# Layer 0's modulation additions redistributed over TensorE, VectorE and w_out, unused columns left unsplit, and the last head's maximum placed ahead of a split

## The reference

```
for l in range(2):
    mod = silu(c) @ w_ada[l] + b_ada[l]                 # 2048 x 6144
    shift, scale, gate = split(mod, 3)
    h = layernorm(x) * (1 + scale) + shift
    u_f, z_f, cq, ckv, k_r, z_a = split(h @ w_in[l])
    y_f = fourier_mix(u_f, w_fmix[l]) * silu(z_f)       # 8 groups of 128
    q, k, v from rmsnorm(cq) @ w_q_b[l], rmsnorm(ckv) @ w_kv_b[l], rope
    y_a = softmax(q k / sqrt(192)) v * silu(z_a)        # 8 heads
    y = concat(y_f, y_a) @ w_out[l]
    x = layernorm(alpha * x + gate * y, ln_g[l], ln_b[l])
```

## Time and profile before

| | |
|---|---|
| Median of 3 runs | 2102.82 us (2100.85 to 2103.71) |
| The profiled execution | 2105.26 us, its span 2103.5 us |
| PE busy | 96% of the span |
| DVE busy | 66% |
| ACT busy | 44% |
| DMA | 219 GB/s from and to HBM over the span |
| Layer 0, from its last Fourier groups to the turn into layer 1 | about 200 to 478 us of the span |

### The profile page before, as it was taken

The page is one execution under the profiler, slowest core; times in us unless marked ns, Lnnn a source line. Parts: engine busy times, 40 slices in busy tenths (PEclk is TensorE's granted clock), DMA queues, the critical chain, the costliest instruction groups (busy, mean ns, idle before and its releaser), DMA issues.

```text
span 2103.5 us, 36631 instructions
## 1 busy us (share of the span) xinstructions
PE 2026.9 (96%) x14264; PEld 1842.2 (88%) x14264; DVE 1378.0 (66%) x1891; ACT 934.9 (44%) x1390; POOL 29.7 (1%) x59
## 2 busy tenths in 40 slices
PE   5999999988999999899999999999999999999998
PEld 1788898768999987899999998889889889989986
DVE  5457677786788867888997555565455545545555
ACT  2344455444545644433346335454334434434443
POOL 0000000000000000000000000000000000000000
PEclk8999999999999999999999999999999999999999
DMA  9988888874577565344545555544545555555553
GB/s 366 397 332 315 311 317 312 320 260 172 199 258 256 224 219 196 122 180 168 184 168 181 201 184 194 200 159 181 200 181 184 195 195 184 180 199 182 190 189 138
DMA packets 64403, 462.40 MB, mean 220 GB/s; under 512 B 7264, under 2 KB 7808, under 8 KB 8368
## 3 DMA queue, kind: packets, MB, share of 16 engines
q1 hardware_dynamic: 57152, 410.49, 53.1%
q0 software_dynamic: 7152, 50.51, 6.5%
HBM read 458.85 MB, written 2.13 MB: 219 GB/s over the span
## 4 chain that ended last, share of the span: by engine, by line
PE 68%; DVE 7%; ACT 2%; issue 1%; DVEq 0%; ACTq 0%
PE ps L523 22%; PE ps L524 22%; PE ps L525 22%; DVE w_lo L1697 2%; DVE area L1733 1%; ACT w_hi L1149 1%; PE ps L565 1%; DVE st L1717 1%; ACT sc L1403 0%; ACT sc L1409 0%; DVE X L2174 0%; DVE grow L2271 0%; DVE csil L2118 0%; DVE area L2271 0%; ACT area L1531 0%
## 5 line engine op out<-in xcount | busy, mean ns | idle before, releaser
L1697 DVE TENSOR_TENSOR w_lo<-raw,w_hi 128x1024 fp32r<-128x1024 f32 x642 | 758.5, 1221 | 390.0 <-ACT w_hi L1149 387.0
L1149 ACT CAST w_hi<-raw 128x1024 fp32r<-128x1024 f32 (+1 forms) x642 | 640.8, 1047 | 457.3 <-PE ps L525 440.8
L523 PE MATMUL ps<-a_hi,w_lo 128*128 128x256 f32 (+1 forms) x2912 | 826.1, 284 | 10.0 <-DVE w_lo L1697 3.7
L524 PE MATMUL ps<-a_lo,w_hi 128*128 128x256 f32 (+1 forms) x2912 | 822.3, 282 | 0.0
L525 PE MATMUL ps<-a_hi,w_hi 128*128 128x256 f32 (+1 forms) x2912 | 821.2, 282 | 0.0
L523 PEld LDWEIGHTS ps<-a_hi,w_lo 128*128 128x128 f32 x2912 | 550.3, 189 | 38.3 <-issue 33.3
L525 PEld LDWEIGHTS ps<-a_hi,w_hi 128*128 128x128 f32 x2912 | 550.6, 189 | 0.0
L524 PEld LDWEIGHTS ps<-a_lo,w_hi 128*128 128x128 f32 x2912 | 547.7, 188 | 0.6 <-issue 0.5
L523 PE MATMUL ps<-w_hi,y_lo 128*128 128x512 f32 x720 | 282.1, 392 | 3.2 <-DVE w_lo L1697 3.2
L525 PE MATMUL ps<-w_hi,y_hi 128*128 128x512 f32 x720 | 280.9, 390 | 0.0
L524 PE MATMUL ps<-w_lo,y_hi 128*128 128x512 f32 x720 | 280.8, 390 | 0.0
(11 more groups left out here) (274 smaller groups left out, 2049.5 us busy)
## 6 DMA issues: line engine op xcount, KB each, us to landing
raw<-in_stream SPq DMA_DIRECT2D x331, 1024.0 KB, 4.8
area<-in_ada SPq DMA_DIRECT2D x46, 1024.0 KB, 7.5
area<-in_ada POOLq DMA_DIRECT2D x40, 1024.0 KB, 5.6
grow<-in_ada SPq DMA_DIRECT2D x10, 1024.0 KB, 6.3
area<-in_rows POOLq DMA_DIRECT2D x4, 1024.0 KB, 7.0
X<-in_x SPq DMA_DIRECT2D x1, 2048.0 KB, 9.5
grow<-row_scratch POOLq DMA_DIRECT2D x2, 1024.0 KB, 7.4
grow<-in_rows POOLq DMA_DIRECT2D x2, 1024.0 KB, 4.9
```

Source lines behind the costliest of these rows:

```text
L523: pe.matmul(o, w[1], a[0], start=first, stop=False, skip_group_check=shared)
L524: pe.matmul(o, w[0], a[1], start=False, stop=False, skip_group_check=shared)
L1149: ac.copy(to, raw[:, bass.ds((g % RAW) * CH + h * n, n)]).then_inc(hi_ready, 1)
L1697: ve.tensor_tensor(to, raw[:, bass.ds((g % RAW) * CH + h * n, n)], hi.bitcast(F32), ALU.subtract).then_inc(lo_ready, 1)
```

## The change

1. TensorE makes 22 additions in place of 24. In the Fourier groups those after `L_FOUR` + 11, 13 and 15 are gone; the heads keep their 11; w_out has five (after chunks 1, 4, 7, 9, 11) where it had four (3, 6, 9, 11). The slots follow two lists now (`PE_GROW`, `PE_AREA`).
2. VectorE makes 26 in place of 24. The two new ones (chunks 13 and 15 of the gate row) stand in groups 6 and 7, behind `gate`; GpSimd loads them into the middle third of `area`. Every count of `ada_step` rises by 2 behind them.
3. VectorE's seven additions in w_out follow chunks 0, 2, 5, 6, 9, 10 and 12 in place of 0, 2, 4, 5, 7, 8 and 10. The one after "12" stands behind `z_block(2, 1)`. TensorE's `finish_rows(4)` stands behind q = 2 in place of q = 1.
4. Of a chunk's second half only the used columns are split: 512 of 1024 in the head projections, 256 in the chunk with w_fmix. This holds in both layers.
5. In the last head of each layer the maximum is taken ahead of the split of the z_a side's next chunk and of the last product's rest.

```diff
-PE_ADDS = tuple(L_FOUR + i for i in (6, 8, 9, 10, 11, 12, 13, 14, 15)) \
+PE_ADDS = tuple(L_FOUR + i for i in (6, 8, 9, 10, 12, 14)) \
     + tuple(L_HEAD + i for i in (1, 3, 4, 5, 7, 8, 10, 11, 12, 14, 15)) \
-    + tuple(L_OUT + i for i in (3, 6, 9, 11))
-PE_BEFORE = {i: i - 2 for i in range(2, 21)} | {i: i - 1 for i in range(21, 24)}
-W_ADDS = (0, 2, 4, 5, 7, 8, 10)
+    + tuple(L_OUT + i for i in (1, 4, 7, 9, 11))
+PE_GROW = (1, 3, 4, 5, 6, 8, 10, 12, 14, 16)
+PE_AREA = tuple(i for i in range(len(PE_ADDS)) if i not in PE_GROW)
+PE_BEFORE = {b: a for s in (PE_GROW, PE_AREA[:2], PE_AREA[2:]) for a, b in zip(s, s[1:])}
+DVE_MORE = 2
+W_ADDS = (0, 2, 5, 6, 9, 10, 12)
...
+def second_half(g):
+
+    o = g % PER_LAYER if isinstance(g, int) and g < B2_MIX else -1
+    if o == L_FMIX:
+        return HALF // 4
+    return HALF // 2 if L_HEAD <= o < L_OUT and (o - L_HEAD) % 2 == 0 else HALF
...
+def pe_row_chunk(i):
+
+    return 2 * i + 1 if i < KT // 2 - DVE_MORE else 2 * (i + DVE_MORE) + 1
...
             for i in range(1, 3 * KT // 2):
-                pool.wait_ge(ada_step, i)
+                pool.wait_ge(ada_step, i + max(0, min(i - 7, DVE_MORE)))
                 weights(2 * i, 0)
+                if i == 6:
+                    pool.wait_ge(ada_pe, 3)
+                    weights(13, 1)
+                if i == 7:
+                    pool.wait_ge(ada_step, 8)
+                    weights(15, 1)
...
             for par, r in enumerate((R_LNG, R_LNB)):
-                pool.wait_ge((ada_step, ada_pe)[par], 3 * KT // 2)
+                pool.wait_ge((ada_step, ada_pe)[par], 3 * KT // 2 + (DVE_MORE, -DVE_MORE)[par])
                 row((lng, lnb)[par], r, aff_in)
...
             def finish_rows(r, added=True):
 
-                pe.wait_ge(ada_step, KT // 2 * (r - 1) if added else 5 * KT // 2)
+                pe.wait_ge(ada_step, DVE_MORE + (KT // 2 * (r - 1) if added else 5 * KT // 2))
...
                     later(L_OUT + 12 + q)
-                    if l == 0 and q == 1:
+                    if l == 0 and q == 2:
                         finish_rows(4)
...
                     gate(q, bank(1))
                     if l:
-                        add_ada(n + 1, 1, n + 1 - KT * 3 // 2)
+                        add_ada(n + 1, 1, n + 1 - KT * 3 // 2 + DVE_MORE)
+                    elif q > 5:
+                        add_ada(2 * q + 1, 1, 2 * q - 5)
                     early(g + 3)
                     t_part(q)
...
-                    after(g + 1, g0 + 1)
-                    if not first:
-                        y_rest(GROUPS + h - 1)
+                    if h < HEADS - 1:
+                        after(g + 1, g0 + 1)
+                        if not first:
+                            y_rest(GROUPS + h - 1)
 
                     ve.wait_ge(s_ps, 8 * l + h + 1)
                     own.link(ve.tensor_reduce(stat[:, 0:2], bank(5, 0, 2 * T).rearrange("p (q k) -> p q k", q=2),
                                               AX.X, ALU.max))
                     ve.tensor_scalar(stat[:, 2:4], stat[:, 0:2], -SM_SCALE, None, ALU.mult).then_inc(s_max, 1)
+                    if h == HEADS - 1:
+                        after(g + 1, g0 + 1)
+                        y_rest(GROUPS + h - 1)
...
                 z_block(2, 0)
                 last_split(g + 12, 3, False)
                 z_block(2, 1)
+                ada_in_w_out(12)
```

More of the change, by code:

```diff
@@ L291, in pe_slot @@
         def pe_slot(i):
-            return grow[:, :] if i % 2 and i < 20 else area[:, CH:2 * CH]
+            return grow[:, :] if i in PE_GROW else area[:, CH:2 * CH]
         lng, lnb = area[:, 0:D], area[:, D:2 * D]
@@ L430, in _ @@
                     row_weights(1)
+                if g == L_HEAD + 4:
+                    sp.wait_ge(ada_step, KT // 2 + DVE_MORE)
+                    row_weights(7)
                 for i, before in PE_BEFORE.items():
@@ L480, in _ @@
                 if i == KT + 1:
-                    pool.wait_ge(ada_pe, 20)
+                    pool.wait_ge(ada_pe, PE_GROW[-1] + 1)
                     gate_everywhere(0)
@@ L705, in a_tok, with ada_add @@
                 return a_hi[:, at:at + P], a_lo[:, at:at + P]
-            def ada_add(n):
+            def ada_add(i):
+                n = pe_row_chunk(i)
                 r = 2 + n // KT
@@ L715, in ada_add @@
                     pe.wait_ge(gate_row, 1)
-                i = n // 2
-                pe.wait_ge(ada_rowed[i % 2], 16 * (i // 2 + 1))
+                own_ = PE_GROW if i in PE_GROW else PE_AREA
+                pe.wait_ge(ada_rowed[i in PE_GROW], 16 * (own_.index(i) + 1))
                 for j in range(4):
@@ L2052, in group @@
                         n = 3 * KT + 2 * (q - 4)
[L2053 removed]
+                        add_ada(n, 0, n - KT * 3 // 2 + DVE_MORE, 5 if q == 4 else 0)
                     else:
[L2055 removed]
+                        add_ada(2 * q, 0, q + (q == 7))
                     early(g + 2)
```

35 lines of the change are left out of this document (18 added, 17 removed).

## The result

The changed kernel takes 2111.98 us (median of 5 executions, 2109.65 to 2114.68) beside 2102.82 us for the kernel before: a ratio of 1.0039, 95% interval 1.0026 to 1.0051. It is slower by 9.2 us. (The quotient of the two medians is 1.0044; ratios and intervals are given here as they were measured, and are not that quotient.) The forecast was 2106.0 us with a range of 2100 to 2112. The direction was right. Of the three verdicts the forecast gave most weight to "within 0.2%" (0.53); what came is "slower" (0.36), the case of rival B, which stood at 2109.3 us.

A forecast was written before the change was run, and what follows sets the result against it. PE, busy for 96% of the span, was taken as the bound. Layer 0's gains are swallowed by w_out's late end (+3.75 us), layer 1 gives -0.50: +3.25 us, 2102.8 + 3.2 = 2106.0 us, range 2100 to 2112.

The forecast's parts named there:

- rival B: w_out's second half: contended loads make the same chain later, slower beyond 0.2%, +6.5 us, 2109.3 us; chance 0.36.
- Part 1: PE's additions: 0.97 us each, two fewer give -1.94 us; -2.91 up to the heads, +0.97 in w_out.
- Part 2: Group 7: PE waits at finish_rows(2) for VectorE's last row-2 addition, +2.35 us; half clock up to 1.7 more, left to range.
- Part 4: Head projections, unused columns: shorter splits that PE does not wait for, taken as 0; remote bound 2.7 us.
- Part 5: Last head of each layer: earlier maximum removes waits, -1.34 us in layer 0 and -0.50 in layer 1.
- Part 3: w_out: late split goes, -3.24 and -1.72 us; PE then stands 6.6 us at finish_rows(4) for the last addition.
- ln_g and ln_b: End of w_out: loads issued late, ln_b landing in 5.9 us sets z_block(3, 1) at 471.95, 3.75 us later.
- The sum: Whole kernel: +3.75 us at z_block(3, 1), layer 0's gains swallowed, -0.50 in layer 1, together +3.25 us.
- The loads: 1 MB loads issued by GpSimd: 6.8 to 7.6 us in the rows, 7.4 taken behind chunk 9; skill's fit 4.4.
- rival C: Group 7 wait eats the saved additions, fast landings leave w_out's end unmoved: -1 to +1 us, 2101.8 to 2103.8; chance 0.15.

The follow-up runs named there:

- e9_fill_group7: Changed kernel with three matmuls of constants ahead of the wait at finish_rows(2); 2111.24 us, ratio 1.0037 to the kernel before.
- a2_after_again: The changed kernel itself, unchanged, in a second set of executions; 2112.64 us, ratio 1.0043 to the kernel before.
- e7_parts_1_2: Changed kernel with parts 3, 4 and 5 taken back; 2104.78 us, ratio 1.0003 to the kernel before.
- e3_parts_4_5: Kernel before with parts 4 and 5 of the change alone; 2101.80 us, ratio 0.9990 to the kernel before.
- e8_spread: Changed kernel with finish_rows(2) behind the first head's projection and VectorE's w_out additions after chunks 0, 2, 3, 5, 6, 8, 10; 2100.16 us, ratio 0.9981.
- e11_add_between: Changed kernel with finish_rows(2) behind the first projection and VectorE's w_out additions after 0, 2, 4, 5, 7, 9, 11; 2097.46 us, ratio 0.9980.
- e12_ln_b_first: e11_add_between with ln_b's load in w_out issued ahead of ln_g's; 2096.80 us, ratio 0.9968 to the kernel before.

## Why the prediction was right, and where it was not

The prediction had the sign, the two places and nearly their waits. That the time falls inside the range is luck, since 3.3 us of the loss in the profile come from a place that it did not think of. Step by step:

- **Part 1.** An addition less was to save 0.97 us. From the common event to where PE is ready for `finish_rows(2)` the changed kernel saves (244.57 - 153.18) - (243.45 - 2.48 - 152.99) = 3.41 us with three fewer, 1.1 us for one. Mis-sized, to the safe side.
- **Part 2.** PE was to wait 2.35 us at `finish_rows(2)`: 2.48 us. Right. "Were the standing to halve the clock ... I leave that to the range": here is the first term that failed. It halved it, and that cost 2.9 us in this profile (e9_fill_group7 is 2.8 us ahead of it behind group 7), more than the 1.7 us allowed; in a2_after_again, with half clock in a part of that stretch only, it cost 1.6, and in e7_parts_1_2 1.5.
- **Part 4** was to move nothing. PE waited in layer 1's heads as before (3.1 us in total, seven times), so that is right; with part 5 the wait for the low half in w_out shrank by 1.37 us in e3_parts_4_5, of which nothing was in the sum.
- **Part 5.** -1.34 and -0.50: both waits are gone, -1.46 and -0.50. Right.
- **Part 3.** The wait for the low half went, as said. At chunk 6 VectorE stood 2.4 us for its load where 3 was forecast. The load behind chunk 9 was sized at 7.4 us and landed in about 5.9 (used at 439.73, VectorE stood 1.65 us, not 3); in the other kernels with the same w_out it took 5.1 to 7.5 us. PE was to stand 6.6 us at `finish_rows(4)`: 6.19. Its wait ended at 455.57 where 454.55 was forecast for the addition's end. (Rival B says that w_out's second half has 12 loads of w_ada where there were 11; these are the numbers for all of w_out.)
- **ln_g and ln_b.** That ln_b would set `z_block(3, 1)`, ahead of PE, was right, and it is what the table of distances shows. Its landing was sized at 5.9 us and took 6.8. From there to `z_block(3, 1)` the forecast had 10.65 us, the runs 10.36.
- **The sum.** +3.75 us at the turn: measured +5.48. Of the 1.7 us missing, 1.1 us are the last addition, which ended later although its load came sooner, since PE, which it follows, came late out of group 7 (without the half clock there the addition came 2.3 us earlier, e9_fill_group7; in a2_after_again PE came out of group 7 1.2 us earlier, but the load took 6.9 us and the addition ended when it did here), and 0.9 us ln_b's landing, less 0.3 for the rest of the chain. In layer 1 -0.50 was forecast: +0.90, since half clock behind the turn lasts over 8.8 us in place of the 3.9 us before. In the feed-forward part 0 was forecast: +3.33, as told above. Together 1.7 + 1.4 + 3.3 = 6.4 us are missing from a sum of 3.25, and 3.25 + 6.4 = 9.7.

So the chain of waits was right and the clock was mis-sized. The prediction counted one stretch of half clock that the change would remove (1.72 us) and none that it would bring, although it forecast two new waits of 2.4 and 6.6 us, and the row of before that it used had half clock behind a wait of 3.24 us. Rival B had the price in it, only for one place and as a matter of bad luck. With half clock in group 7 counted at the 1.72 us of that row, the sum is 3.25 + 1.72 = 4.97 us, which is past 0.2%: B would have been the forecast, if by little. But one row is a thin ground: the runs show waits of 2.3 to 2.7 us without half clock behind them (e7_parts_1_2, e8_spread), so the right form of the term was a chance and a price.

**The loads.** In the Trainium skill, "DMA: Bandwidth & Descriptors", section "Anatomy of one DMA", gives about 4.4 us for 1 MB, an estimate from its fit. The loads of this place landed in 5.9 and 6.8 us in the changed kernel, and the last of ln_g and ln_b in 11.0 and 12.5 us in e11_add_between and e12_ln_b_first, with the weight stream beside them. The prediction was right not to go by the fit, and rival C, which did, is out. The prediction's own 7.4 us for the load behind chunk 9 was as far off as the fit, 1.5 us, on the other side.

## What to carry to other kernels

A new wait of the bound engine can cost more than its length: price the clock behind it as well, as a chance with a price, from all rows of the same trace that show waits of that size, and ask whether the engine can be given other work first (`finish_rows(2)` behind one projection took 5.3 us away for nothing). Where a step is made late so that another runs early, follow what is issued only when it has ended: here two loads of 1 MB behind the last addition set the end of the layer. And several edits that each shorten the same wait do not add up.
